# A transformer layer on one core: the recurrence's gate products on 64 by 64 quarters of TensorE's array

## The reference, cut to what matters

```python
ub = u.reshape(B_, L, LRU_BLOCKS, LRU_BLOCK_W)                # 8 blocks of 64 channels
r = jax.nn.sigmoid(jnp.einsum('blnc,ncd->blnd', ub, w_a).reshape(B_, L, D_LRU) + b_a)
i = jax.nn.sigmoid(jnp.einsum('blnc,ncd->blnd', ub, w_x).reshape(B_, L, D_LRU) + b_x)
log_a = (-LRU_C * jax.nn.softplus(-lam)) * r
a = jnp.exp(log_a)
b = jnp.sqrt(-jnp.expm1(2.0 * log_a)) * (i * u)
_, h = lax.associative_scan(_linear_combine, (a, b), axis=1)   # both directions, context first
```

## Time and profile before

| | |
|---|---|
| median of three timed runs | 2221.43 us (2220.92 to 2223.82) |
| profiled execution | 2228.47 us |
| its span | 2226.4 us, 43616 instructions |
| TensorE busy | 2116.1 us, 95% |
| VectorE, ScalarE, GpSimd busy | 1002.1, 389.9, 395.7 us |
| mean granted clock of TensorE | 0.975 of full speed |
| products of line 744 | 96 instructions, first at 74.4 us, last at 305.7 us |

### The profile page before, as it was taken

How to read it: one execution, slowest core, us unless ns; L and a number is a source line. 1 busy time by engine, 2 the same in 40 slices (tenths; PEclk the granted TensorE clock), 3 DMA queues, 4 the chain that set the end, 5 groups by cost and what they waited for, 6 DMA issues and landing times.

```text
span 2226.4 us, 43616 instructions
## 1 busy us (share of the span) xinstructions
PE 2116.1 (95%) x14127; PEld 875.2 (39%) x14128; DVE 1002.1 (45%) x1509; ACT 389.9 (18%) x553; POOL 395.7 (18%) x399
## 2 busy tenths in 40 slices
PE   6999999789979999999999999999999999999995
PEld 3544444464553343433333333333333333534332
DVE  2665655666676333333233333434244245243345
ACT  2344347331220000000000000000010001000032
POOL 1011100101222111211112212122121221222102
PEclk9999999889969999999999999999999999999998
DMA  9312321012253757667579869696697887979985
GB/s 349 97 58 76 113 67 29 1 77 98 85 220 133 270 191 264 241 223 276 182 302 367 302 248 364 253 363 249 242 357 295 325 319 290 367 279 403 322 309 206
DMA packets 153781, 512.70 MB, mean 230 GB/s; under 512 B 17248, under 2 KB 51684, under 8 KB 136202
## 3 DMA queue, kind: packets, MB, share of 16 engines
q1 hardware_dynamic: 135138, 464.77, 53.8%
q0 software_dynamic: 15840, 37.87, 7.7%
q10 hardware_dynamic: 2760, 9.48, 1.1%
HBM read 482.08 MB, written 32.51 MB: 231 GB/s over the span
## 4 chain that ended last, share of the span: by engine, by line
PE 85%; DVE 8%; issue 2%; DMA 2%; SPq 1%; ACT 1%; DVEq 0%; POOLq 0%; POOL 0%; another core or an unknown queue 0%
PE psall L591 42%; PE psall L624 13%; PE psall L777 9%; PE psall L628 5%; PE psall L765 3%; PE psall L884 2%; PE psall L878 2%; PE psall L634 2%; PE psall L744 1%; SPq L448 1%; DVE arena L1511 1%; DVE arena L1665 1%; PE psall L697 1%; PE psall L910 1%; DMA arena<-in_w_up_dram 1%
## 5 line engine op out<-in xcount | busy, mean ns | idle before, releaser
L591 PE MATMUL psall<-arena 128*32 128x512 f32 x9216 | 1003.4, 593 | 10.6 <-issue 4.3
L591 PEld LDWEIGHTS psall<-arena 128*32 128x32 f32 x9216 | 326.2, 110 | 678.1 <-issue 664.2
L1683 DVE STREAM_TRANSPOSE arena<-arena 128x1024 f32<-128x1024 f32 x48 | 59.8, 1246 | 645.0 <-PE psall L591 639.7
L624 PE MATMUL psall<-arena 128*128 128x512 f32 x736 | 321.9, 595 | 10.6 <-DVE arena L1740 9.3
L1283 ACT ACTIVATE arena<-arena 128x1024 f32<-128x1024 f32 x49 | 51.8, 1058 | 1259.1 <-DVE arena L1711 1259.1
L777 PE MATMUL psall<-arena 128*128 128x512 f32 (+1 forms) x560 | 227.1, 562 | 0.0
L624 PEld LDWEIGHTS psall<-arena 128*128 128x128 f32 x736 | 137.9, 190 | 195.2 <-issue 180.6
L1665 DVE TENSOR_TENSOR arena<-psall,arena 32x256 f32<-32x256 f32 (+2 forms) x122 | 78.6, 645 | 235.7 <-PE psall L624 124.3
L2057 POOL DMA_INDIRECT arena<-h_rows,lruw x144 | 149.1, 1035 | 85.0 <-POOL lruw L2050 38.4
L777 PEld LDWEIGHTS psall<-arena 128*128 128x128 f32 x560 | 106.3, 190 | 109.1 <-issue 106.1
L628 PE MATMUL psall<-arena 128*64 128x512 f32 x576 | 127.6, 595 | 0.0
(11 more groups left out here) (357 smaller groups left out, 1676.8 us busy)
## 6 DMA issues: line engine op xcount, KB each, us to landing
arena<-in_w_gate_dram SPq DMA_DIRECT2D x128, 1024.0 KB
arena<-in_w_up_dram SPq DMA_DIRECT2D x128, 1024.0 KB
arena<-in_w_down_dram SPq DMA_DIRECT2D x128, 1024.0 KB
arena<-in_w_ada_dram SPq DMA_DIRECT2D x16, 1024.0 KB, 5.2
arena<-in_w_ada_dram SPq DMA_DIRECT2D x4, 2048.0 KB, 14.7
arena<-in_x_dram SPq DMA_DIRECT2D x16, 512.0 KB, 7.0
arena<-in_w_in_dram SPq DMA_DIRECT2D x16, 512.0 KB, 4.0
arena<-in_w_out_dram SPq DMA_DIRECT2D x1, 4096.0 KB, 13.8
```

The costliest lines, as they stand in the source:

```text
L591: mm = pe.matmul(sums[QR * j:QR * j + QR, t], rows[:, k, QR * t:QR * t + QR], wpair[m][:, :, k % 2, QW * j:QW * j + QW], start=(k == 0), s ...
L624: mm = pe.matmul(ps[6 + s], aT[:, k, :], w[:, s * BANK:(s + 1) * BANK], start=(k == 0), stop=(k == KD - 1))
```

## The change

The gate products of the two long segments no longer use the whole 128 by 128 array with zero blocks. Each segment is two products of 64 by 64 by 512: the channels of half h (partitions 64h to 64h + 63) by the half's own matrix. Half h goes to bank 5 + h. Segment 0 leaves half h in the partitions of half h; segment 1 leaves it in the other half (`gate_rows`). So the four products of both segments lie on the four quarters of the array. `lru_mm` is counted up by the second product of each segment. ScalarE takes each segment with two ACTIVATEs of 64 partitions by 512, and counts `lru_sig` up with the second. TensorE waits before the first product for the second sigmoid of the gate before, not only for the first. The third segment is as before, and its two waits are now written apart.

```diff
@@ -424,6 +424,9 @@
             return 2 * pr * (NS - 1) + before_ + STATE_GROUPS[g].index(n) + 1
 
 
+        def gate_rows(b, h):
+            return slice(HT * ((h + b) % 2), HT * ((h + b) % 2) + HT)
+
         def chunked(ap):
             return ap.rearrange("p (a b i) -> p b a i", a=4, b=KD)
 
@@ -736,13 +739,22 @@
                     pe.wait_ge((proj_act, proj_dve)[e], cnt)
                     if i == 0 and not g:
                         pe.wait_ge(d_lruw, 16 * 12)
-                    for b, (s0, s1) in enumerate(segs_all):
-                        if 2 * i + g:
-                            pe.wait_ge(lru_sig, 3 * (2 * i + g - 1) + b + 1)
-                            if b == 2 and 2 * i + g > 1:
-                                pe.wait_ge(adarow_done, 2 * i + g - 1)
-                        pe.matmul(ps[JB + b][:, 0:s1 - s0], lruw[:, (d * 2 + g) * JL + j, :], XL[:, j, s0:s1],
-                                  start=True, stop=True).then_inc(lru_mm, 1)
+                    w = (d * 2 + g) * JL + j
+                    if 2 * i + g:
+                        pe.wait_ge(lru_sig, 3 * (2 * i + g - 1) + 2)
+                    for b, (s0, s1) in enumerate(segs_lat):
+                        for h in range(2):
+                            rows = slice(HT * h, HT * h + HT)
+                            mm = pe.matmul(ps[JB + h][gate_rows(b, h), :], lruw[rows, w, HT * h:HT * h + HT], XL[rows, j, s0:s1],
+                                           start=True, stop=True, skip_group_check=True)
+                        mm.then_inc(lru_mm, 1)
+                    if 2 * i + g:
+                        pe.wait_ge(lru_sig, 3 * (2 * i + g - 1) + 3)
+                    if 2 * i + g > 1:
+                        pe.wait_ge(adarow_done, 2 * i + g - 1)
+                    s0, s1 = segs_all[2]
+                    pe.matmul(ps[JB + 2][:, 0:s1 - s0], lruw[:, w, :], XL[:, j, s0:s1],
+                              start=True, stop=True).then_inc(lru_mm, 1)
                 if what == "ada":
                     if i == 0:
                         continue
@@ -1100,10 +1112,18 @@
                         act.wait_ge(lru_done, i)
                     if i == 0 and not g:
                         act.wait_ge(proj_done, 3)
-                    for b, (s0, s1) in enumerate(segs_all):
+                    at = (C_BA, C_BX)[g] + d * JL + j
+                    for b, (s0, s1) in enumerate(segs_lat):
                         act.wait_ge(lru_mm, 3 * (2 * i + g) + b + 1)
-                        act.activation((lB, lC)[g][:, s0:s1], ps[JB + b][:, 0:s1 - s0], ACT.Sigmoid,
-                                       bias=par[:, (C_BA, C_BX)[g] + d * JL + j:(C_BA, C_BX)[g] + d * JL + j + 1]).then_inc(lru_sig, 1)
+                        for h in range(2):
+                            rows = slice(HT * h, HT * h + HT)
+                            done = act.activation((lB, lC)[g][rows, s0:s1], ps[JB + h][gate_rows(b, h), :], ACT.Sigmoid,
+                                                  bias=par[rows, at:at + 1])
+                        done.then_inc(lru_sig, 1)
+                    s0, s1 = segs_all[2]
+                    act.wait_ge(lru_mm, 3 * (2 * i + g) + 3)
+                    act.activation((lB, lC)[g][:, s0:s1], ps[JB + 2][:, 0:s1 - s0], ACT.Sigmoid,
+                                   bias=par[:, at:at + 1]).then_inc(lru_sig, 1)
                 elif what == "decay":
                     j, d = i // 2, i % 2
                     act.wait_ge(lru_sig, 6 * i + 6)
```

## The result

| | us |
|---|---|
| before, median of 10 | 2221.93 (2219.82 to 2223.82) |
| changed, median of 10 | 2228.56 (2226.78 to 2230.41) |
| ratio | 1.0028 (95%: 1.0020 to 1.0037) |
| changed, profiled execution | 2229.64, span 2227.7 |

What follows compares the result with a forecast made beforehand. TensorE was taken as the bound (busy 2116.1 of 2226.4 us), with sigmoids last at some gates. Terms -0.54 + 1.08 + 1.16 + 0.20 - 2.70 - 0.48 + 1.05 gave -0.23 us: 2221.2 us, range 2218 to 2225 (with rivals 2214.5 to 2227).

Steps and rivals of the forecast that it cites:

- r0, i0, r1: gate_r and gate_i of step 0, gate_r of step 1: -0.54, +1.08 and +1.16 us, the last two from longer sigmoids.
- i1, r2: gate_i of step 1, gate_r of step 2: 1.16 us of sigmoids exceed a slack of 0.96, so +0.20 us.
- i2 and i3: gate_i of steps 2 and 3: two long TensorE jobs behind each cover the sigmoids, so -0.54 us each.
- r3, i4, r4, r5: gate_r of steps 3 to 5: sigmoid chain becomes the bound, -0.12 us each; gate_i of step 4: -0.54 us.
- i5, r6's short product: gate_i of step 5, gate_r of step 6: longer sigmoids delay the short product at 253.82 us, +1.05 us.
- The products: Gate products on TensorE: eight quarters, four at once, save 0.86 us; tile-shape switch costs 0.32; net 0.54 us per gate.
- The sigmoids: Line 1105 on ScalarE: half-partition ACTIVATEs keep the 0.58 us distance of whole ones, adding 1.16 us per gate.
- Who waits: Sum products (line 753) wait for all three sigmoids of their gate; going gate by gate sums to -0.23 us.
- waits that let the clock fall: Rival, TensorE's longer waits before 112.54 us and at r6: each 5 us at 1.2 GHz costs 2.5 us; 2223.7-2226.2 us, 8%.
- Free halves: Rival, sigmoids on ScalarE: half-partition ACTIVATEs cost nothing extra, gaining 6.4 us, 2215.1 us; chance 13%.
- pairs of quarters: Rival, gate products on TensorE: quarters run only two at a time, costing 7.1 us, 2228.6 us; chance 6%.
- ScalarE last in every gate: Rival, all 16 gates: ScalarE's 1.16 us on the path against 0.54 gained, +9.9 us, 2231.3 us; chance 3%.

Runs made afterwards that it cites:

- e2: Kernel before with its whole-array products, but each long segment's sigmoid taken as two halves of 64 partitions: +7.5 us against before, ratio 1.0037.
- e5: Kernel before with half-partition sigmoids, lower halves of both long segments first, then the upper ones: +11.2 us against before, one run.
- e1: Changed kernel's quarter products, but each long segment's sigmoid as one whole 128x512 ACTIVATE (gate values wrong): 5.7 us under before, ratio 0.9974.
- e4: Changed kernel, short segment's sigmoid first in gate_r gates, the sum product behind waiting for that one alone: 3.9 us under before, ratio 0.9987.
- e16: Changed kernel with idle products filling three long TensorE waits (before the sum products of i0 and r1, and r6's short product): +4.9 us against before, ratio 1.0019.
- e10: Changed kernel, short segment first in gate_r gates, with i0, r1 and i5 back on whole-array products and whole sigmoids: 8.4 us under before, ratio 0.9966.

## Why the prediction was wrong

By its own steps, the difference of the chain of waits between sum products, after less before. The first part begins with r0's product, at 74.97 us in both. Each ends at a sum product, except the fifth and the sixth, which meet at r6's short product:

| part | forecast | measured | why |
|---|---|---|---|
| r0, i0, r1 (to 112.5 us) | +1.70 | +3.33 | pitch of the halves twice (0.96), clock 0.6 |
| i1, r2 | +0.20 | +2.18 | pitch 0.48, clock 1.7, less 0.16 |
| i2 and i3 | -1.08 | -0.52 | 0.50 each, less 0.24 of restart each |
| r3, i4, r4, r5 | -0.90 | +0.36 | pitch three times and a restart, less 0.16 three times |
| i5, r6's short product (to 253.8) | +1.05 | +1.85 | pitch, restart |
| to 264.3, i6, r7, i7 | -1.20 | -0.38 | pitch once, restart |
| sum | -0.23 | +6.82 | |

Pitch is the distance of the sigmoids from start to start: 1.64 us more for a gate than before, not 1.16. A restart is the longer sum product behind a wait. The clock's 0.6 is what is left of the first part when the rest is taken off. The 0.16 is my error of reading: the chain beside r3 is 8.00 us from the chain's start of the sum product (165.17), not 8.16, and r2's slack is 0.16 more by the same reading (141.99, not 141.83).

*The products.* Right. 0.86 us less and 0.32 for the switch were forecast; the chain has 1.02 + 0.63 us for a gate, 0.50 under the 2.15 of the earlier trace rows (forecast 0.54). So the eight quarters take 0.16 us more than two rounds, and the short product behind them 0.20 more than its 0.43: 0.36 for the switch. The rule of the Trainium skill (TensorEngine Tiling (Array Packing), Key Properties) that a change of mode drains TensorE agrees with that price; no run here tells a drain from another cost of the change, such as a weight load that is no longer hidden.

*The sigmoids.* Here the first step failed: "With half the partitions I expect the same 0.58: a COPY of 2x512 out of the banks takes 576 ns". That row is one instruction's duration; what I needed was the distance between two. It was right that the duration does not depend on the partitions (682 ns against 684), but the distance is 0.70. The 0.12 of overlap is lost four times, the last time between the last half and the short segment. A gate's sigmoids are 2 x 0.58 + 4 x 0.12 = 1.64 us longer, not 1.16. I had named a bound of 1.58, from 4 x 0.684, and its price in the sum, +3.4 us; but I took the optimistic end, and even the bound was 0.06 short. Eight gates have ScalarE on the path: 8 x 0.48 = 3.8 us. It is the term of the sum that was mis-sized, and e2 and e5 show it.

*Who waits.* The eight places were right, and every one showed as a wait: r3's chain was forecast to be the bound and was. e1 and e4 bear it out: there the gates from r3 to r5 give their 0.50 us each. My wait at r1 was too long (3.9 us, measured 3.25), because a part of it had moved to i0, whose wait grew from 0.80 to 2.83 us; I had not named that one. What I left out was that a sum product after a wait takes 0.24 us more on the chain, five times, 1.2 us; the row for it stood before me (0.67 at 112.54 against 0.43 in others).

*The clock.* The rival "waits that let the clock fall" got 8%, and it came on top of the forecast. I had named a granted clock under 1.00 between 50 and 400 us as a sign of being wrong. Its price was right in size (+2.5 us for 5 us at 1.2 GHz; 1.7 us for one fall, near 2.4 in all by e16), its chance was not: I read it from the broken work after 420 us and had no row on long waits in dense work. The profiles of the runs have them: behind waits of up to 2.32 us between 50 and 410 us the clock never fell, behind 18 waits of 2.33 to 3.76 us it fell 16 times (not behind 3.08 us in the first profile of the changed kernel, nor behind one of 2.77 in e5). That is a count of these runs and no limit: the same wait of 3.08 us came out both ways.

*The rivals.* Free halves and pairs of quarters are out by the rows. *ScalarE last in every gate*, the Trainium skill's page TensorEngine Tiling (Array Packing), PSUM Bottleneck, was nearer to the truth than I gave it (3%): not in every gate, but most of what was lost was indeed lost in emptying the banks. On the range: each error alone stays under its top of 2227.0 us (+3.4 gives 2224.6, +2.5 to +5.0 gives 2223.7 to 2226.2), both together do not (2227.1 to 2229.6). I took them for rivals of each other, but they had one cause, since a longer sigmoid makes the longer wait that the clock falls behind.

## What to carry to other kernels

Before dividing an evacuation by partitions, look at the distance between neighbouring instructions, not at the duration of one: here halves of columns cost 0.14 us a segment more, halves of partitions 0.82. A faster product is worth what the chain beside it leaves; list for each wait what ends last, and use the fast form only where TensorE is the bound (the mixed kernel: 8.4 us faster than before with quarters in 13 of the 16 gates and the short segment first, where quarters in all 16 had made it 6.6 us slower). A wait that grows can also cost the clock behind it (here 1.7 us where TensorE was the bound behind the wait, 0.6 where VectorE was), so its price is not linear.

## What the runs showed that was not expected

ScalarE overlaps an ACTIVATE with the one before by about 0.1 us (0.59 from start to start for 0.68 of duration) only where the first partition read and the first one written both stay: two halves on the same 64 partitions overlap like whole ones, and a change of either gave 0.68 to 0.71 us. The number of partitions may change. In e4 and e10 a short sigmoid on all 128 is followed by one on the lower 64, and the overlap is kept: 0.37 us from start to start for 0.47 of duration (e4, timeline of ScalarE at 169 us).

```profile
169.03 0.47 ACT L1119 ACTIVATE arena<-psall,par 128x256 f32<-128x256 f32 x1 [1.73 <-DVE arena L1463]
169.40 2.77 ACT L1127 ACTIVATE arena<-psall,par 64x512 f32<-64x512 f32 x4
```

TensorE's granted clock went to 1.2 GHz behind single waits, the shortest of 2.33 us, in the midst of otherwise dense work. When the first two such waits were filled with idle products, it fell behind the third, where it had not in the first profile.
